# Attention mixers of two layers run as 40 steps with their projections, norms and rotations placed between the steps

## The reference

```python
def _token_mixers(h, w_in, sink, ..., w_out, layer_idx):
    proj = h @ w_in
    a, b, c, d = jnp.split(proj, [A_COLS, A_COLS + B_COLS, A_COLS + B_COLS + C_COLS], axis=-1)
    o_a = _mixer_window(a, sink, slopes[:WIN_HEADS])          # 4 heads, keys within 128, distance bias, a sink
    o_b = _mixer_mla(b, mla_q_norm, mla_w_uq, mla_kv_norm, mla_w_ukv, pos)   # 4 heads from normed latents, rotary on 32
    o_c = _mixer_axial(c, ax_q_norm, ax_k_norm)               # 4 heads, q and k normed, rotary on 64
    o_d = _mixer_diff(d, diff_lambda, diff_subln, slopes[WIN_HEADS:], layer_idx)
    return jnp.concatenate([o_a, o_b, o_c, o_d], axis=-1) @ w_out

    # of _mixer_diff, for each of 4 heads and both halves m of q and k:
        s = jnp.einsum('bqhmd,bkhmd->bhmqk', qi, k).astype(jnp.float32) * scale + bias[None, :, None]
        p = jax.nn.softmax(s, axis=-1)
        w = p[:, :, 0] - lam * p[:, :, 1]
        return jnp.einsum('bhqk,bkhd->bqhd', w.astype(v.dtype), v)
    o = _rms_norm(o, subln_g) * (1.0 - lam_init)
```

## Time and profile before

| what | value |
|---|---|
| median of 3 runs | 3706.17 us (3704.44 to 3746.83) |
| profiled execution, its time | 3726.48 us |
| its span in the trace | 3724.2 us |
| TensorE busy, share of the span | 95% |
| VectorE, ScalarE | 49%, 38% |
| mean granted TensorE clock | 0.948 of full speed |

### The profile page before, as it was taken

The page is one execution under the profiler, slowest core; times in us unless marked ns, Lnnn a source line. Parts: engine busy times, 40 slices in busy tenths (PEclk is TensorE's granted clock), DMA queues, the critical chain, the costliest instruction groups (busy, mean ns, idle before and its releaser), DMA issues.

```text
span 3724.2 us, 47651 instructions
## 1 busy us (share of the span) xinstructions
PE 3529.4 (95%) x17300; PEld 2894.8 (78%) x17300; DVE 1839.8 (49%) x2694; ACT 1415.8 (38%) x2269; POOL 11.1 (0%) x13
## 2 busy tenths in 40 slices
PE   7988799999799999999999999999999999989997
PEld 6857688887688888888766688888888876678886
DVE  4576666535566534333464463335333455553335
ACT  3341344324544324222445442324232445433323
POOL 0000000000000000000000000000000000000000
PEclk9999999999899999999989599999999999589998
DMA  3210122222222322222210022222222220013233
GB/s 125 83 51 1 53 88 99 95 92 81 73 85 96 99 89 99 98 97 91 86 45 1 18 74 96 96 97 91 97 96 97 86 73 1 1 49 104 96 100 100
DMA packets 89742, 288.51 MB, mean 77 GB/s; under 512 B 9968, under 2 KB 14576, under 8 KB 89072
## 3 DMA queue, kind: packets, MB, share of 16 engines
q1 hardware_dynamic: 89440, 284.69, 22.9%
q0 software_dynamic: 144, 1.70, 0.1%
HBM read 284.26 MB, written 2.10 MB: 77 GB/s over the span
## 4 chain that ended last, share of the span: by engine, by line
PE 87%; DVE 7%; ACT 3%; issue 2%; DMA 1%; DVEq 0%; ACTq 0%; SPq 0%
PE gb L528 23%; PE gb L529 23%; PE gb L530 23%; PE gb L1034 4%; PE pm L1063 3%; PE pm L1050 2%; DMA wst<-in_weights 1%; PE gb L849 1%; DVE wl L1646 1%; DVE rinv L1676 1%; PE gb L589 1%; PE gb L588 1%; PE gb L590 1%; PE pm L858 1%; ACT h L1171 1%
## 5 line engine op out<-in xcount | busy, mean ns | idle before, releaser
L528 PE MATMUL gb<-xh,wh 128*128 128x512 f32 (+1 forms) x3264 | 1223.1, 375 | 85.9 <-DVE xl L1700 31.6
L529 PE MATMUL gb<-xl,wh 128*128 128x512 f32 (+1 forms) x3264 | 1209.1, 370 | 0.0
L530 PE MATMUL gb<-xh,wl 128*128 128x512 f32 (+1 forms) x3264 | 1208.3, 370 | 0.0
L1646 DVE TENSOR_TENSOR wl<-wst,wh 128x1024 fp32r<-128x1024 f32 (+3 forms) x600 | 647.3, 1092 | 557.7 <-ACT wh L1121 551.0
L1121 ACT CAST wh<-wst 128x1024 fp32r<-128x1024 f32 (+3 forms) x600 | 557.6, 943 | 638.0 <-DMA wst<-in_weights 637.7
L528 PEld LDWEIGHTS gb<-xh,wh 128*128 128x128 f32 x3264 | 626.4, 192 | 203.3 <-issue 39.6
L529 PEld LDWEIGHTS gb<-xl,wh 128*128 128x128 f32 x3264 | 627.3, 192 | 103.1 <-issue 2.2
L530 PEld LDWEIGHTS gb<-xh,wl 128*128 128x128 f32 x3264 | 627.0, 192 | 101.6
L528 PE MATMUL gb<-hid,wh 128*128 128x512 f32 (+2 forms) x1212 | 447.0, 369 | 2.8 <-DVE wl L1646 2.8
L530 PE MATMUL gb<-hid,wl 128*128 128x512 f32 (+2 forms) x1212 | 443.7, 366 | 0.0
L529 PE MATMUL gb<-hid,wh 128*128 128x512 f32 (+2 forms) x1212 | 443.6, 366 | 0.0
(11 more groups left out here) (340 smaller groups left out, 2970.1 us busy)
## 6 DMA issues: line engine op xcount, KB each, us to landing
wst<-in_weights SPq DMA_DIRECT2D x408, 512.0 KB, 3.3
wst<-in_weights SPq DMA_DIRECT2D x84, 384.0 KB, 2.9
wst<-in_weights SPq DMA_DIRECT2D x84, 320.0 KB, 2.9
h<-in_x_t SPq DMA_DIRECT2D x2, 1024.0 KB, 6.2
out_t<-h SPq DMA_DIRECT2D x8, 256.0 KB, 2.3
tab<-in_first SPq DMA_DIRECT2D x1, 1984.0 KB, 15.1
wst<-in_weights SPq DMA_DIRECT2D x20, 96.0 KB, 2.1
tab<-in_second POOLq DMA_DIRECT2D x1, 1664.0 KB, 7.3
```

The costliest lines, as they stand in the source:

```text
L528: pe.matmul(dst, w_hi, x_hi, start=start, stop=False)
L529: pe.matmul(dst, w_hi, x_lo, start=False, stop=False)
L530: return pe.matmul(dst, w_lo, x_hi, start=False, stop=stop)
L1646: dve.tensor_tensor(wl[:, s, m, a], wst[:, s, m, a], f32(wh[:, s, m, a]), ALU.subtract).then_inc(lo_split, 1)
```

## The change

The 80 units become 40 steps of two score matrices each, in the order diff, ax, win, mla. A diff step holds both halves of one head, so every second diff step has a turn (transposes of two heads); all other steps have one each, 32 turns in all. The score pair goes to two neighbouring banks (`gb[:, 2:4]`); banks 0 and 1 now belong to the projections, which are cut to 64 parts (`PARTS`, `PER_STEP`) and stand between the score and value products of the steps. ScalarE copies finished banks out at steps given by `EVICT_AT`; the norms, rotary swaps and weight splits stand at steps given by their own tables. In the value product the values are the stationary operand (64 columns) and the turned scores move, the two heads writing partitions 0 to 63 and 64 to 127 of one bank, so the result is feature-major already: `features` and `divide` are gone. In their place VectorE multiplies the scores of both heads by the reciprocal of their sums before the transposes. Bias tables are read with a scale in the instruction instead of being multiplied out by ScalarE. The first chunk of the output projection stands among the last four steps. Weight columns and the packing follow the new order.

```diff
+STEPS = [("diff", p_, qt_, e_) for p_ in range(2) for qt_ in range(NT) for e_ in range(2)]
+STEPS += [(kind_, p_, qt_, None) for kind_ in ("ax", "win", "mla") for p_ in range(2) for qt_ in range(NT)]
+NS, NTURN = len(STEPS), 32
+TURN_OF = [s_ // 2 if s_ < 16 else s_ - 8 for s_ in range(NS)]
+LAST = [2 * t_ + 1 if t_ < 8 else t_ + 8 for t_ in range(NTURN)]
+EVICTS = 28
+PART_COUNT = {c_: 8 for c_ in range(2, 9)} | {9: 2, 10: 2, 11: 1, 12: 1, 13: 2}
+PER_STEP = [4, 4, 3, 3, 2] + [2] * 12 + [3, 3, 2] * 2 + [2, 0, 2, 1, 1, 0, 2] + [0] * 10
+ALL_PARTS = [(c_, i_) for c_ in range(2, 14) for i_ in range(PART_COUNT[c_])]
+PARTS = [ALL_PARTS[sum(PER_STEP[:s_]):sum(PER_STEP[:s_ + 1])] for s_ in range(NS)]
+EVICT_AT = {1: ((2, 0),), 2: ((2, 1),), 4: ((3, 0),), 5: ((3, 1),), 7: ((4, 0),), 9: ((4, 1),), 11: ((5, 0),), 13: ((5, 1),),
+            15: ((6, 0),), 17: ((6, 1),), 19: ((7, 0),), 20: ((7, 1),), 22: ((8, 0),), 23: ((8, 1),)}
+EVICT_AT |= {u_: ((c_, 0), (c_, 1)) for u_, c_ in ((24, 9), (26, 10), (27, 11), (28, 12), (30, 13))}
+SPLIT_STEP = {0: 3, 3: 4, 6: 5, 10: 6, 14: 7, 18: 8, 21: 9, 24: 10, 25: 11, 27: 12, 28: 13, 30: 14, 32: 15}
+DQ, DK, VD, VWA, AQ, AK, KR, CQ, CKV, WK, WQ, MQ = 0, 2, 4, 6, 8, 10, 11, 12, 14, 15, 16, 18
+E_SLOT, PT_SLOT, Y_SLOT, SUB_SLOT, LAT_HI, LAT_LO = 22, 30, 34, 37, 38, 41
+MK, MV, SWAP_SLOT = DQ, VD, MQ + 2
+AX_SQ_AT, AX_SUM_AT, AX_ROOT_AT, AX_NORM_AT = {5: 0, 6: 1, 8: 2}, {6: 0, 8: 1, 10: 2}, {7: 0, 9: 1, 11: 2}, {8: 0, 10: 1, 12: 2}
+SWAP_AT, ROTATE_AT = {5: 0, 7: 1, 9: 2, 11: 3, 25: 4, 26: 5, 27: 6, 28: 7}, {6: 0, 8: 1, 10: 2, 12: 3, 26: 4, 27: 5, 28: 6, 29: 7}
+SUB_SUM_AT, SUB_ROOT_AT, SUB_NORM_AT = {12: 0, 20: 1}, {13: 0, 21: 1}, {14: 0, 22: 1}
+ML_SUM_AT, ML_ROOT_AT, ML_NORM_AT = {18: 0, 21: 1}, {19: 0, 22: 1}, {20: 0, 23: 1}
+Y_STEP = {LAST[4 * y_ + 3] + 5: y_ for y_ in range(8)}
...
+def score_banks(s):
+
+    return 0 if STEPS[s][0] == "mla" and s % 2 == 0 else 2
...
+                def scores(s):
+
+                    kind, p, qt, e = STEPS[s]
+                    if kind == "mla" and s >= 34:
+                        q("exp_done", NS, s - 1)
+                    elif kind == "mla":
+                        q("max_ready", NS, 32)
+                    elif s >= 1:
...
+                        q("kr_copied", 4, 4)
+                    k0, k1 = keys(kind, qt)
+                    for i in range(2):
+                        lhs, rhs = operands(s, i)
+                        mm = pe.matmul(gb[:, score_banks(s) + i, 0:(k1 - k0) * P], lhs[:, qt * P:(qt + 1) * P], rhs[:, k0 * P:k1 * P],
+                                       start=True, stop=True)
+                    mm.then_inc(S("s_done"), 1)
+
+                def turn(t):
+
+                    kind, p, qt, e = STEPS[LAST[t]]
+                    k0, k1 = keys(kind, qt)
+                    q("p_dve", NS, LAST[t] + 1)
+                    q("pt_copied", NTURN, t)
+                    pe.sem_inc(S("pe_waited"), 1)
+                    for i, src in enumerate(turned(t)):
+                        for j in range(k1 - k0):
+                            mm = pe.transpose(pm[:, i, j * P:(j + 1) * P], src[:, j * P:(j + 1) * P], IDENT)
+                    mm.then_inc(S("pt_done"), 1)
...
+                    pe.sem_inc(S("pe_waited"), 1)
+                    for j in range(k0, k1):
+                        for i in range(2):
+                            mm = pe.matmul(mixed[64 * i:64 * i + 64, qt * P:(qt + 1) * P], value(kind, p, i, j),
+                                           pt_slots(t)[:, i, (j - k0) * P:(j - k0 + 1) * P], start=j == k0, stop=j == k1 - 1)
+                    mm.then_inc(S("v_done"), 1)
+
...
+                two_by_half(c0, n - 1, l)
+                for u in range(NS + 4):
+                    if u < NS:
+                        ahead = (len(PARTS[u]) + 1) // 2
+                        projected = [k for k in PARTS[u] if k[0] < 9]
+                        for c, i in projected[:ahead]:
+                            part_of(c, i)
+                        scores(u)
+                        for c, i in projected[ahead:]:
+                            part_of(c, i)
+                    else:
+                        for k in ((0, 1), (2, 3), (4, 5), (6,))[u - NS]:
+                            out_part(k)
+                    if u - 4 in LAST:
+                        values(LAST.index(u - 4))
+                    if u - 2 in LAST:
+                        turn(LAST.index(u - 2))
+                    for c, i in PARTS[u] if u < NS else ():
+                        if c >= 9:
+                            part_of(c, i)
+                    if u in AX_SUM_AT:
+                        axial_sum(AX_SUM_AT[u])
+                    if u in SWAP_AT:
+                        swap(SWAP_AT[u])
+                    if u in SUB_SUM_AT:
+                        sub_sum(SUB_SUM_AT[u])
+                    if u in ML_SUM_AT:
+                        latent_sum(ML_SUM_AT[u])
+                out_part(KT - 1)
+                q("exp_done", NS, NS)
+                residual_out(c0 + 14, None, n, l, 2 + l)
...
-                for u in range(NU + L_PAIR):
-                    if u < NU:
-                        scores(u)
-                    if u in ROPE_STEP:
-                        swap(ROPE_STEP[u])
-                    v = u - L_TURN
-                    if 0 <= v < NU and is_turned(v):
-                        turn(v)
-                    v = u - L_VALUES
-                    if 0 <= v < NU and is_turned(v):
-                        values(v)
-                    v = u - L_PAIR
-                    if v >= 0:
-                        y, last = head_pair(v)
...
+                for u in range(NS + 5):
+                    if u in Y_STEP:
+                        take(Y_STEP[u])
+                    if u - 3 in LAST:
+                        copy_turned(LAST.index(u - 3))
...
+                    if u in AX_ROOT_AT:
+                        f = AX_ROOT_AT[u]
+                        q("ax_sum", 3, f + 1)
+                        scale, bias = (1.0, eps_c[:, :]) if f < 2 else (1.0 / 64, eps_of[EPS_LN])
+                        act.activation(ax_tmp(f), misc, ACT.Sqrt, scale=scale, bias=bias).then_inc(S("ax_rt"), 1)
...
+                    if u < NS:
                         exponentials(u)
...
+                def maxima(s):
+
+                    kind, p, qt, e = STEPS[s]
+                    k0, k1 = keys(kind, qt)
+                    w = (k1 - k0) * P
+                    small, b = small_of(s), score_banks(s)
+                    q("s_done", NS, s + 1)
+                    if kind not in BIASED:
+                        dve.reduce_max(small[:, 0:2], gb[:, b:b + 2, :], AX, negate=True).then_inc(S("max_ready"), 1)
...
+                def sums(s):
+
+                    kind, p, qt, e = STEPS[s]
+                    k0, k1 = keys(kind, qt)
+                    w = (k1 - k0) * P
+                    small = small_of(s)
+                    q("exp_done", NS, s + 1)
+                    total = 2
+                    if kind == "win":
+                        m2.then(dve.tensor_tensor(small[:, 10:12], small[:, 2:4], small[:, 6:8], ALU.add))
+                        total = 10
+                    if kind == "diff":
+                        m2.then(dve.reciprocal(small[:, 8:10], small[:, 2:4]))
+                        m2.then(dve.tensor_scalar(small[:, 12:13], small[:, 2:3], sm[:, 20, 5:6], small[:, 9:10], ALU.mult, ALU.mult))
+                        m2.then(dve.scalar_tensor_tensor(e_slot(s, 1), e_slot(s, 1), small[:, 12:13], e_slot(s, 0), ALU.mult, ALU.add))
+                        ins = dve.tensor_scalar(e_slot(s, 1), e_slot(s, 1), small[:, 8:9], None, ALU.mult)
+                    else:
+                        m2.then(dve.reciprocal(small[:, 8:10], small[:, total:total + 2]))
+                        for i in range(2):
+                            ins = dve.tensor_scalar(e_slot(s, i)[:, 0:w], e_slot(s, i)[:, 0:w], small[:, 8 + i:9 + i], None, ALU.mult)
+                    ins.then_inc(S("p_dve"), 1)
...
+                def axial(f):
+                    q("ax_rt", 3, f + 1)
+                    m2.then(dve.reciprocal(ax_tmp(f), ax_tmp(f)))
+                    dve.tensor_tensor(slot(AQ + f), slot(AQ + f), ax_tmp(f), ALU.mult).then_inc(S("ax_normed"), 1)
+
...
+                for u in range(NS + 5):
+                    if u in ROTATE_AT:
+                        rotate(ROTATE_AT[u])
+                    if u in AX_NORM_AT:
+                        axial(AX_NORM_AT[u])
+                    if u in SUB_NORM_AT:
+                        sub_norm(SUB_NORM_AT[u])
+                    if u in ML_NORM_AT:
+                        latent_norm(ML_NORM_AT[u])
+                    if u < NS:
+                        maxima(u)
+                    if 1 <= u <= NS:
+                        sums(u - 1)
+                    if Y_STEP.get(u, 0) >= 3:
+                        low_y(Y_STEP[u])
+                    if u in (22, 25):
```

791 lines of the change are left out of this document (382 added, 409 removed).

## The result

The changed kernel takes 3602.27 us (median of 4, 3597.11 to 3604.52); the kernel before, run beside it, 3726.5 (median of 4, 3704.44 to 3770.97). The ratio is 0.973, 95% interval 0.969 to 0.977: faster by 2.7%. The kernel before scatters: in this and three later sessions its medians were 3726.5, 3706.0, 3720.0 and 3701.3 us, and its 37 runs together go from 3673.91 to 3770.97 with 3704.4 in the middle. Its shorter runs show the higher granted clock (.967 at 3673.91 us, .954 at 3705.98, .946 at 3726.13). Two of the seven runs behind the 3720.0 are marked slow; the other five have a median of 3702.3. The changed kernel, repeated in another session, gave 3603.27. Against the middle of all runs of the kernel before, the gain is 102 us or 2.8%.

A forecast was written before the change was run, and what follows sets the result against it. TensorE was taken to bound the attention. Per layer, 221 us of its work plus 38 of waits gave 259 against 323, 64 less, 128 for both: 3578 us from the median of 3706.2; range 3520 to 3665.

The forecast's parts named there:

- Layer stretch 259 us: From the end of chunks 0 and 1 to the end of chunk 14: 259 us a layer against 323.
- TensorE's work, 221: One layer at full clock: projections 95.6, scores 45.5, transposes 25.5, values 36, swaps 7.4, chunk 14 10.9; 221 us.
- (a): Steps 8, 10, 12, and norms of 14, 20, 22, 23: TensorE waits for VectorE's rotations, norms and maxima, 9 us.
- (b): Win steps 24 to 31: VectorE's 39 us and ScalarE's 36 exceed TensorE's 32, so 8 us of waits.
- (c): Win steps: granted clock 0.75 as in the earlier win stretch, a third more on 32 us, 11 us.
- (d): Every step: handovers between engines, 0.15 us a step, 6 us.
- (e): Start of mla, and the last value's way to the output projection (copy, low part): 4 us.
- (1): Values run side by side with little waiting: 231 us a layer, 92 less, 3522 us; chance 0.17.
- (2): Steps in lockstep, each costing its busiest engine's work, no slack carried over: 286 us a layer, 3632; chance 0.15.
- (3): Value products: weight loads aren't hidden, a turn costs 2.55 us instead of 1.66; 3654 us; chance 0.06.
- (4): Mixed steps 0 to 23: half clock slows the projections too, 86 us more a layer, 3878; chance 0.09.
- (5): Norm roots: each table switch costs 1.4 us more on the path, 19 us a layer, 3616; chance 0.03.

The follow-up runs named there:

- best_b: Changed kernel with chunk 12's split in step 26, norms by exp and ln, and splits of chunks 14 and 15 moved to steps 37 and 41: 3553.1 us.
- norms_log: Changed kernel with 1/sqrt of the seven norms per layer made on ScalarE as exp(-.5 ln x), without VectorE's reciprocals: 3582.8 us.
- unmixed: Changed kernel with projection chunks 2 to 8 done ahead of the 40 steps, so steps 0 to 22 hold only attention work: 3700.9 us.

## Why the prediction was right, and where it was off

The time of 3602.3 lies in the range and on the forecast's side. The point, 3578, is 24 us low, and 20 of that come from one step: the 128 us were the difference to a profiled execution of 3726.5 us, whose granted clock of .948 is lower than that of most runs (.954 in the middle), and they were taken off a median of 3706. The 259 us a layer belong to 3598, which the prediction also names, and 3602.3 was measured. The 3706 itself was not low: 3704.4 is the middle of all runs. That the sum of a layer fits so well is luck in part, as the terms show.

- **Layer stretch 259 us:** 264.0 and 258.2.
- **TensorE's work, 221:** 226 in best_b, where the clock is full. By the start times there: scores 46.0, values 30.9, transposes 26.4, and 8.7 for seven swaps and the two sums of squares of the diff norm. These two sums, some 1.8 us, had no term; the other six sums of squares are already in the 95.6 (L951 and L980 stand in that stretch of the kernel before). With 95.6 and 10.9 this makes 218.5. The other 7.4 us are the price of the mixed order itself, which the prediction put at nothing: at a change between projection products and others, a product takes about .1 us longer, at some 80 places. The values were taken at 36, the middle, where they came near to side by side, so errors of -5 and +9 us leave the sum 5 low. Scores side by side at 1.05: the runs show it, and that parting them costs 1.0 each. The change of kind, in the changed kernel ahead of and behind the scores of step 6:

```profile
1848.41 0.40 PE L550 MATMUL gb<-xh,wl 128*128 128x512 f32 x1
1848.73 1.13 PE L1049 MATMUL gb<-work_a 32*128 32x512 f32 x4
1849.79 0.50 PE L548 MATMUL gb<-xh,wh 128*128 128x512 f32 x1
1850.13 0.39 PE L549 MATMUL gb<-xl,wh 128*128 128x512 f32 x1
```

The product ahead of the scores takes .32 and the one behind them .34, where inside a part it is .23.

- **(a) Norms, 9 us:** 9.8 by norms_log. The places, steps 9, 11 and 13, were right. Of the 8.0 in diff 3.5 are these waits; the rest is another gap of 1.2 and the half clock, 3.3. Step 14 has no wait, and the norms of steps 20, 22 and 23 gave 1.8 in ax.
- **(b) and (c), win, 19 us:** 18.4 in layer 0 and 12.4 in layer 1, over 32 of work. By busy time this is 7.7 idle and 11 of half clock in layer 0, just the terms 8 and 11, and 10.5 and 2 in layer 1. The sum fits one layer, the reasons don't. (b) put the idle time down to 39 us of VectorE's work and 36 of ScalarE's; they are busy for 32 and 27. 4.2 of the idle time is a wait that the prediction didn't have: the split of chunk 12 in the step that needs it, to be read from the table of splits beside that of parts. With it gone win takes 40.0 us, and with the splits of 14 and 15 moved too, 36.6, at 1.00. So the .75 taken over from the win stretch of the earlier trace rows was no property of the win steps, and the fit of (c) in layer 0 is luck.
- **(d) Handovers, 6 us:** no view has them apart. TensorE's queue had work left at most handovers, and best_b, with 40 of them, has 10 us between busy time and span in all.
- **(e) Start of mla and the last value, 4 us:** too low. The last value's wait of 1.4 is there. The copies of turned tiles stood behind splits 14 and 15 on ScalarE; moving these gave 6.7 us in each layer, half of it in win.
- **Full clock in mixed steps:** .97 to 1.00, as expected. By the estimate above the clock is the larger part of what went (37 us against 33 of work in layer 0). But the parts don't stand alone: unmixed has the lower work and half of the clock's loss gone, and loses both again in idle time. Why the clock stays up in the mixed steps is not shown; no run keeps the cover and lowers the clock.
- **VectorE 175, ScalarE 170:** 171 and 155. The normalising product took .484, not .428.

The rivals. (1) was right on the values, wrong on little waiting and on what the mixed order costs TensorE. (2) lockstep falls for the changed kernel, whose diff steps keep TensorE busy for 97.8 of 102.5 us, but describes the unmixed one. (3) falls: a turn of 16 loads and 16 products takes 1.02 us, and the trace has loads for .85 of it, so weight loads under products that use the same rows are hidden, in the new layout as in the earlier trace rows. The sentence of the Trainium skill on row groups ("TensorE: Matmul & The Clock Gate", section "What overlaps and what doesn't") does not hold for these products. (4) falls with the clock of the mixed steps. (5) falls: a table load takes 1.28 us as in the earlier trace rows, and ScalarE has room. The 2.66 us of the Trainium skill ("ScalarE: Activation LUTs", section "What ACT_TABLE_LOAD costs") are not seen at the loads in the mixers: the next activation starts .01 to .10 us behind the load, save where it waits for VectorE.

What stays open: how long the half clock behind the 4.2 us wait lasts. In layer 0 of the first profile and of norms_log the win steps took 50.4 and 50.3 us (clock .74), in both layers of the repeat 44.4 (.93 and .94), with the same wait. Open too is what a fuller clock alone would have given the kernel before, whose diff heads lost 40 us a layer to it; no run tried that.

## What to carry to other kernels

Put independent projection products between attention steps when VectorE's chain is as long as TensorE's work: here the gain was gone without it, and filler in place of useful work gave none. Count some .1 us for each change of kind in TensorE's queue. Lay neighbours in the queue on different row or column groups, since the order alone was worth 46 and 11 us. Then read each wait of TensorE in the new order and compare the table of preparations (splits, roots, copies) with that of uses: three numbers moved in a table and a reciprocal taken off VectorE gave 49 us more, beside the 102 to 124 of the restructuring. And take a difference found in one profiled execution off the time of that execution, not off a median.

## What the hardware did that was not expected

Two column groups of 64 run nearly side by side: .51 us for four float32 value products (64 columns loaded, 128 moving), against .76 in the other order. Changing between projection products and others cost TensorE about .1 us each time. In diff steps that were busy to 95%, whose longest wait was 1.85 us, TensorE ran at 1.2 GHz for some microseconds twice, 1.8 us behind that wait and 1.3 behind a gap of 1.2; this is 3.3 of the 8 us that the norms cost the diff steps, and in norms_log, without the waits, the clock stays at 1.00. And behind the same wait of 4.2 us the half clock lasted 23 us in one layer of an execution and 3 us in the other.
